# Cached latent pages on two halves of the stationary columns, with half-page transfers

## The reference

```python
# page: 128 positions; 32 pages for each of 8 samples; 16 heads; latent 256, rotary 32
ckv_past = cache_ckv[layer, page_table].reshape(bd, past, KV_LORA)
kr_past = cache_krope[layer, page_table].reshape(bd, past, QK_ROPE)
s_past = latent_scores(q_lat, q_rope, ckv_past, kr_past)   # (q_lat.ckv + q_rope.kr) * SCALE
s_new = latent_scores(q_lat, q_rope, c_kv, k_rope)         # the sample's own token
p = softmax(concatenate([s_past, s_new], axis=-1))
out = einsum(p[..., :past], ckv_past) + einsum(p[..., past:], c_kv)
```

## Time and profile before

| | |
|---|---|
| median of three runs | 938.44 us |
| profiled execution | 938.16 us, its span 936.5 us |
| TensorE busy | 896.2 us (96%) |
| VectorE, ScalarE, GpSimd busy | 481.7, 253.6, 97.0 us |
| DMA | 247.54 MB, mean 264 GB/s |
| mean granted TensorE clock | 0.991 |

### The profile page before, as it was taken

The page is one execution under the profiler, slowest core; times in us unless marked ns, Lnnn a source line. Parts: engine busy times, 40 slices in busy tenths (PEclk is TensorE's granted clock), DMA queues, the critical chain, the costliest instruction groups (busy, mean ns, idle before and its releaser), DMA issues.

```text
span 936.5 us, 13966 instructions
## 1 busy us (share of the span) xinstructions
PE 896.2 (96%) x5209; PEld 533.3 (57%) x5209; DVE 481.7 (51%) x1084; ACT 253.6 (27%) x553; POOL 97.0 (10%) x146
## 2 busy tenths in 40 slices
PE   8999999999999999999999999899999898897897
PEld 7777777677776755655678644444333333333443
DVE  2343778987753248677666446672111211014784
ACT  1122221032254125765720110221111111012346
POOL 0111211212112100000000000011211111011000
PEclk9999999999999999999999999999999999899999
DMA  9976988998897620101241495639999999999601
GB/s 374 363 253 242 340 289 294 324 385 314 286 360 277 241 75 20 49 20 43 99 186 64 185 425 243 237 122 401 425 421 422 425 421 425 424 417 351 239 24 68
DMA packets 65420, 247.54 MB, mean 264 GB/s; under 512 B 11301, under 2 KB 12078, under 8 KB 56358
## 3 DMA queue, kind: packets, MB, share of 16 engines
q1 hardware_dynamic: 46742, 191.41, 52.4%
q0 software_dynamic: 13216, 35.28, 10.2%
q10 hardware_dynamic: 5392, 19.93, 5.5%
HBM read 240.98 MB, written 18.05 MB: 277 GB/s over the span
## 4 chain that ended last, share of the span: by engine, by line
PE 78%; DMA 13%; DVE 5%; ACT 2%; issue 1%; SPq 1%; DVEq 0%; ACTq 0%; POOLq 0%
PE ps L1046 12%; DMA arena<-in_wexp 10%; PE ps L1538 9%; PE ps L997 8%; PE ps L1458 6%; PE ps L1382 4%; PE ps L1560 4%; PE ps L1133 3%; PE ps L1104 3%; PE ps L1218 3%; PE ps L1037 3%; PE ps L1663 2%; PE ps L1242 2%; PE ps L1182 2%; PE ps L1199 2%; PE ps L1108 1%
## 5 line engine op out<-in xcount | busy, mean ns | idle before, releaser
L1046 PE MATMUL ps<-arena 128*128 128x260 f32 x544 | 125.8, 387 | 1.9 <-DMA arena<-in_xT 1.0
L1046 PEld LDWEIGHTS ps<-arena 128*128 128x128 f32 x544 | 101.8, 191 | 22.9 <-issue 4.5
L2083 DVE SCALAR_TENSOR_TENSOR arena<-arena,vec 128x512 f32<-128x512 f32 x120 | 81.8, 746 | 0.0
L997 PE MATMUL ps<-arena 128*128 128x260 f32 x336 | 78.5, 387 | 0.1
L2935 POOL DMA_DIRECT2D arena<-in_kv x96 | 51.9, 542 | 252.1 <-issue 247.9
L2760 DVE TENSOR_TENSOR arena<-ps,arena 128x256 f32<-128x256 f32 x18 | 7.6, 425 | 129.6 <-ACT arena L1933 129.6
L1538 PE MATMUL ps<-arena 128*64 128x512 f32 x288 | 66.4, 615 | 7.3 <-DMA arena<-in_wexp 6.2
L997 PEld LDWEIGHTS ps<-arena 128*128 128x128 f32 x336 | 62.1, 190 | 12.9 <-issue 3.2
L1538 PE MATMUL ps<-arena,con 128*64 128x512 f32 x288 | 65.7, 609 | 3.7 <-DMA arena<-in_wexp 3.7
L1560 PE MATMUL ps<-arena 128*64 128x512 f32 x288 | 65.1, 593 | 3.7 <-DMA arena<-in_wexp 3.7
L1458 PE MATMUL ps<-arena 128*128 128x512 f32 x128 | 58.0, 600 | 0.0
(11 more groups left out here) (415 smaller groups left out, 1305.0 us busy)
## 6 DMA issues: line engine op xcount, KB each, us to landing
arena<-in_wexp SPq DMA_DIRECT2D x26, 2048.0 KB, 24.4
arena<-in_kv SPq DMA_DIRECT2D x160, 272.0 KB, 9.2
arena<-in_wexp SPq DMA_DIRECT2D x36, 1024.0 KB, 27.4
arena<-in_kv POOLq DMA_DIRECT2D x96, 272.0 KB, 7.5
arena<-in_w ACTq DMA_DIRECT2D x35, 512.0 KB, 8.2
arena<-in_wexp SPq DMA_DIRECT2D x16, 512.0 KB, 4.4
arena<-in_wo SPq DMA_DIRECT2D x8, 512.0 KB, 4.5
arena<-in_w_out SPq DMA_DIRECT2D x4, 1024.0 KB, 7.2
```

What stands on the lines that cost most here:

```text
L997: y = mm(ps[:, paired_bank(p, n), 0:TH], left(k), right(k), start=(k == 0), stop=(k == KD // 2 - 1))
L1046: y = mm(ps[:, b + h, 0:TH], w[:, k], xT[:, k, h * TH:(h + 1) * TH], start=(k == 0), stop=(k == KD - 1))
L2083: y = v.scalar_tensor_tensor(out=aT[:, c, 0:NPR], in0=win, scalar=wt, in1=aT[:, c, 0:NPR], op0=ALU.mult, op1=ALU.add)
```

## The change

Four pages of a sample are now laid on two **sides**. The 32 stationary columns of a sample hold its 16 heads twice, in columns 0 to 15 of one variant (side 0) and 16 to 31 of the other (side 1), each with zeros in the other half. Pages 0 and 1 of the four are scored with side 0 and pages 2 and 3 with side 1, into the same 256 columns of PSUM, so rows 0 to 15 of a sample's block hold two pages and rows 16 to 31 the other two. Scores, exponential and transposes are 256 wide. Values give for each row both sides' sums, 512 wide; the wrong half is not used, and the two right halves are added after the turning (`olT`). Each half of the rows has its own maximum and sum; a permutation `swap`, built from the identity by two copies, carries them over in two small matmuls at the end.

A page in memory is now 64 rows of 1088 numbers: row p, the rotary keys of two of the four position blocks each (64 numbers), row 64+p. It comes in two transfers, one to partitions 0 to 63 and one to 64 to 127, of 2048 and 2304 bytes a row; the longer one brings the rotary keys, to the lower partitions for pages 0 and 1 of four and to the upper for pages 2 and 3. So one rotary matmul contracts over the keys of both sides.

The core of the diff:

```diff
+ROW, HALF = 2 * P + KVL, P // 2
+SIDES, HH = 2, 16
...
+        def half_of(j, h):
+            return slice(h * ROW, (h + 1) * ROW + HALF) if h == j % 4 // 2 else slice(h * (ROW + HALF), h * (ROW + HALF) + ROW)
+        def page_half(n, j, h):
+            b, u = divmod(j, 4)
+            x = u // 2
+            first = x * (ROW + HALF)
+            place = slice(first - HALF * x * h, first + ROW + HALF * (1 - x) * (1 - h))
+            return rec[HALF * h:HALF * (h + 1), n % 2, b, u % 2, place]
...
-                    sp.dma_start(rec[:, n % 2, j], a["kv"][bass.ds(pg, 1)].rearrange("a p n -> (a p) n")
-                                 ).then_inc(s_kv[n % 2], 16)
+                    for h in range(2):
+                        sp.dma_start(page_half(n, j, h), a["kv"][bass.ds(pg, 1), :, half_of(j, h)].rearrange("a p n -> (a p) n")
+                                     ).then_inc(s_kv[n % 2], 16)
...
             def k_step(n):
-                pe.wait_ge(s_kv[s], 16 * SPN * (n // 2 + 1))
-                pe.wait_ge(s_kvp[s], 16 * (STEPS - SPN) * (n // 2 + 1))
+                pe.wait_ge(s_kv[s], 32 * SPN * (n // 2 + 1))
+                pe.wait_ge(s_kvp[s], 32 * (STEPS - SPN) * (n // 2 + 1))
                 for c in range(KKV):
+                    for x in range(SIDES):
+                        for bb in range(4):
+                            mm(ps[32 * bb:32 * bb + 32, bank, 0:2 * P], qlat[:, c, x, 4 * r + bb, :],
+                               rec[:, s, bb, :, x * (ROW + HALF) + c * P:x * (ROW + HALF) + (c + 1) * P], start=(c == 0 and x == 0), stop=False)
+                for j in range(2):
                     for bb in range(4):
-                        mm(ps[32 * bb:32 * bb + 32, bank, :], qlat[:, c, 4 * r + bb, :], kvr[:, s, bb, :, c * P:(c + 1) * P],
-                           start=(c == 0), stop=False)
-                for j in range(4):
-                    for bb in range(4):
-                        y = mm(ps[32 * bb:32 * bb + 32, bank, :].rearrange("p (u j i) -> p j u i", u=4, j=4)[:, j],
-                               qrz[:, j, 4 * r + bb, :], kvr[:, s, bb, :, 2 * P:2 * P + 32], start=False, stop=(j == 3))
+                        y = mm(ps[32 * bb:32 * bb + 32, bank, 0:2 * P].rearrange("p (u j i) -> p j u i", u=2, j=2)[:, j],
+                               qrz[:, j, 4 * r + bb, :], rec[:, s, bb, :, ROW:ROW + HALF], start=False, stop=(j == 1))
...
             def k_turn(n):
-                for u in range(4):
+                for u in range(2):
...
             def v_step(n):
-                for u in range(4):
-                    for bb in range(4):
-                        y = mm(ps[32 * bb:32 * bb + 32, 7, 0:KVL], pts[:, s, u * P + 32 * bb:u * P + 32 * bb + 32],
-                               kvr[:, s, bb, u, 2 * P + 32:REC], start=(u == 0), stop=(u == 3))
+                for x in range(SIDES):
+                    for u in range(2):
+                        for bb in range(4):
+                            y = mm(ps[32 * bb:32 * bb + 32, 7, x * KVL:(x + 1) * KVL], pts[:, s, u * P + 32 * bb:u * P + 32 * bb + 32],
+                                   rec[:, s, bb, u, x * (ROW + HALF) + 2 * P:x * (ROW + HALF) + ROW],
+                                   start=(u == 0), stop=(u == 1))
...
             def scores(p, s, x):
-                    pe.wait_ge(s_new, 3)
+                    pe.wait_ge(s_new, 7)
...
             def own_scores(r):
                 if r == 0:
+                    mm(ps[:, 4, 2:4], swap, negm[:].rearrange("p (r g) -> p r g", r=2)[:, :, 7], start=True, stop=True)
...
+                        for x in range(SIDES):
+                            mm(ps[32 * bb:32 * bb + 32, 4, r:r + 1], qlat[:, c, x, b, :],
+                               hT[:, B_CKV + c, NPR + b:NPR + b + 1], start=(c == 0 and x == 0), stop=False)
+            def own_sums():
+                pe.wait_ge(s_new, 5)
+                mm(ps[:, 4, 4:6], swap, fin[:, 10:12], start=True, stop=True).then_inc(s_cs, 1)
...
             def out_turn():
+                for x in range(SIDES):
+                    for r in range(2):
+                        for c in range(KKV):
+                            y = tr(ps[:, 6 + x, (2 * r + c) * P:(2 * r + c + 1) * P],
+                                   osum[r][:, (KKV * x + c) * P:(KKV * x + c + 1) * P], ident)
...
             gen_r(0)
+            own_sums()
             gen_v(0, 0)
...
             summed(STEPS - 1)
+            own_weights()
+            out_r(0, (0,))
             own()
-            out_r(0, (0, 1))
             out_v(0, 0)
...
-                    v.tensor_copy(olT.rearrange("p r c n -> p (r c n)"), ps[:, 6, :]).then_inc(s_olt, 1)
-                    out_r(0, (2, 3))
+                    v.tensor_copy(both, sides[0]).then_inc(s_olt, 1)
+                    dve.wait_ge(s_olt, 1)
+                    v.tensor_tensor(both, sides[1], both, ALU.add).then_inc(s_olt, 1)
+                    out_r(0, (1, 2, 3))
```

More of the change, by code:

```diff
@@ L409, in decoder_layer @@
         qlt = at(A_P, 1024)
[L410 to L420, removed]
+        qlat = at(A_QLAT, SIDES * KKV * NS * 32).rearrange("p (c x b h) -> p c x b h", c=KKV, x=SIDES, b=NS)
+        qrz = at(A_QRZ, 2 * NS * 32).rearrange("p (j b h) -> p j b h", j=2, b=NS)
+        rec = at(A_KV, 2 * STEPS * REC).rearrange("p (s b u n) -> p s b u n", s=2, b=4, u=2)
+        prb = at(A_P, 512).rearrange("p (s n) -> p s n", s=2)
+        pts = at(A_PTS, 512).rearrange("p (s n) -> p s n", s=2)
+        swap = at(A_SWAP, P)
+        osum = [at(off, SIDES * KVL) for off in (A_O, A_O2)]
+        olT = at(A_OLT, 256).rearrange("p (r c n) -> p r c n", r=2, c=KKV)
         wuv = at(A_W1R + 2048, 2048).rearrange("p (c n) -> p c n", c=KKV)
@@ L2048, in _ @@
             v.memset(fin[:], 0.0).then_inc(s_ini, 1)
+            v.memset(krs[:], 0.0).then_inc(s_ini, 1)
             dve.wait_ge(s_ini, N_INI)
@@ L2270, in _ @@
                     for c in range(KKV):
-                        v.tensor_copy(qlat[:, c, :, 0:HEADS].rearrange("p b (j i) -> p b j i", j=4), lat[:, c, 0:NS]
-                                      ).then_inc(s_qd, 1)
+                        for x in range(SIDES):
+                            v.tensor_copy(qlat[:, c, x, :, HH * x:HH * (x + 1)].rearrange("p b (j i) -> p b j i", j=4), lat[:, c, 0:NS]
+                                          ).then_inc(s_qd, 1)
+                    halves = [y.rearrange("p (b x h) -> p b x h", x=SIDES, h=HH) for y in (swap, ident)]
+                    for x in range(SIDES):
+                        v.tensor_copy(halves[0][:, :, x], halves[1][:, :, 1 - x]).then_inc(s_qd, 1)
                 if kind == "pw":
@@ L2381, in out_p, with own_weights @@
                                   ps[:, 5, c0:c0 + (i + 1) * P].rearrange("p (j q) -> p j q", q=P)).then_inc(s_td, 1)
-            def own():
-                last = negm[:].rearrange("p (r g) -> p r g", r=2)[:, :, 7]
-                lpast = lsum[:].rearrange("p (r g) -> p r g", r=2)[:, :, 7]
+            last = negm[:].rearrange("p (r g) -> p r g", r=2)[:, :, 7]
+            lpast = lsum[:].rearrange("p (r g) -> p r g", r=2)[:, :, 7]
+            def own_weights():
                 dve.wait_ge(s_cs, 2)
@@ L2414, in _ @@
+                dve.wait_ge(s_new, 12)
+                for r in range(2):
+                    y = v.scalar_tensor_tensor(out=osum[r][:, 0:KVL], in0=ps[:, 5, r * KVL:(r + 1) * KVL], scalar=fin[:, 16 + r:17 + r],
+                                               in1=osum[r][:, 0:KVL], op0=ALU.mult, op1=ALU.add)
+                y.then_inc(s_fin, 1)
             dve.wait_ge(s_cs, 1)
             v.tensor_copy(ckvs[:], ps[0:NS, 2, 0:KVL]).then_inc(s_cse, 1)
-            v.tensor_copy(krs[:], hT[64:96, B_KR, NPR:T]).then_inc(s_cse, 1)
+            for x in range(SIDES):
+                v.tensor_copy(krs[64 * x:64 * x + 32, :], hT[64:96, B_KR, NPR:T]).then_inc(s_cse, 1)
@@ L2424, in _ @@
                 if p == 0:
-                    dve.wait_ge(s_cs, 3)
-                    v.tensor_copy(olT.rearrange("p r c n -> p (r c n)"), ps[:, 6, :]).then_inc(s_olt, 1)
-                    out_r(0, (2, 3))
+                    dve.wait_ge(s_cs, 4)
+                    sides = [ps[:, 6 + x, :].rearrange("p (n x h) -> p n x h", x=SIDES, h=HH)[:, :, x] for x in range(SIDES)]
+                    both = at(A_OLT, 256).rearrange("p (n h) -> p n h", h=HH)
+                    v.tensor_copy(both, sides[0]).then_inc(s_olt, 1)
+                    dve.wait_ge(s_olt, 1)
+                    v.tensor_tensor(both, sides[1], both, ALU.add).then_inc(s_olt, 1)
+                    out_r(0, (1, 2, 3))
                 else:
@@ L2934, in step_pages @@
                     pg = pool.snap(numbers[j], min_val=0, max_val=NPOOL - 1)
-                    pool.dma_start(rec[:, n % 2, SPN + j], a["kv"][bass.ds(pg, 1)].rearrange("a p n -> (a p) n")
-                                   ).then_inc(s_kvp[n % 2], 16)
+                    for h in range(2):
```

(3 more changed lines are left out.)

73 lines of the change are left out of this document (36 added, 37 removed).

## The result

The changed kernel takes 1007.9 us, the median of four runs (1005.9 to 1015.4), beside 938.3 us (937.7 to 938.5) for the kernel before: 1.076 times as long, with an interval of 1.070 to 1.081. It is 70 us slower. The profiled execution took 1008.39 us.

The account below looks back on a forecast made before the run. Bounds: TensorE's list and, nearly equal behind it, the pages. From 938.2 us, TensorE's steps -13.3 and the own part +4.0 (together -9.3), then +16.9 for late pages, gave 945.8 us; range 928 to 1000 us.

Parts of the forecast that it names:

- The bound: Whole kernel: TensorE busy 96% of the span; behind it the pages, with DMA engines 88% busy from 62 to 320 us.
- serial rival: Page transfers: only one half of the partitions takes bytes at a time, 208 GB/s, 1031 us; chance 0.18, or near.
- the factor for a transfer to 64 partitions: Page transfers: engine time 1.19 times as much, 2.4 us more a step; 1.30 as upper value, giving 961 us.
- slacks: Steps 2 to 15, pages landing before scores start: 0.1 to 5.5 us each; each short by 3.2 us, shortfalls adding 16.9 us.
- TensorE's steps: Sixteen page steps: rotary matmuls save 8.5 us, transposes 4.85 us, together 13.3 us; latent scores and values unchanged.
- The own part: Samples' own row after the last step: 4.0 us added, from scores 1.7, swaps 0.2, transposes 0.6 and VectorE's chain 1.5.
- VectorE's longer chain: Samples' own row: VectorE comes to the second head's rotary products about 1.5 us later than TensorE.
- forecast case: Page transfers at a factor of 1.15 to 1.35, own range 940 to 970 us; chance 0.37.
- faster rival: Page transfers: halves cost the engines nothing, slacks fall short only in steps 6, 7 and 12, 930.6 us; chance 0.35.

Follow-up runs that it names:

- e10: Kernel before, with GpSimd's six pages of sixteen each in three transfers, rows 0 to 63, 64 to 95 and 96 to 127: 966.8 us, ratio 1.033.
- e11: Kernel before, with GpSimd's six pages each in three transfers, rows 32 to 95, 0 to 31 and 96 to 127: 949.2 us, ratio 1.013.
- e3: Kernel before, with only GpSimd's six pages of sixteen cut into two transfers of 64 rows: 973.3 us, ratio 1.037.
- e1: Kernel before, with each page in two transfers of 64 rows of 2176 bytes, nothing else changed: 999.9 us, ratio 1.063.
- e5: Changed kernel, with SyncE bringing the lower halves of all sixteen pages and GpSimd the upper ones: 989.1 us, ratio 1.052 against the kernel before.
- e8: Changed kernel with latents in 128-row transfers, separate rotary keys, eight pages per queue, and no value columns from step 2 on: 927.1 us.
- e9: Kernel before, with pages from step 2 on brought without their 256 value columns: 937.7 us, ratio 0.9991.

## Why the prediction was right and wrong

**The bound, right.** It had two nearly equal bounds, TensorE's list and the pages behind it, and put the cost where it fell: on the DMA engines, in TensorE's idle time before the scores. Most signs it named are there: share 0.97 (0.95 or more was named), landings of 11.2 us in the median on SyncE's queue (8.3 on GpSimd's; 11 and more was named), page packets dearer for a byte (1.42 times in engine time, below), idle time before the scores. But that idle time is 65.7 us and not 15 to 20, and two signs of the serial rival are there too, as told below.

**The step that failed: the factor for a transfer to 64 partitions.** I took 1.19 from one load of eight rows, with 1.30 from a store as the upper value. That load was eight packets in a window of 0.3 us, with a DMA share of 0.33, and it could not stand for queues that are full of half transfers. The store beside it showed 2.9, and I set it aside because pages are loads. Nor does the price go by the number of rows, along which I took the fourth root of 2.9: e10 and e11 have the same rows and differ. In the steps, with the engines full, the factor is 1.4: 360 to 259 GB/s for a unit of engine time over all traffic. For the two queues that bring the pages it is (0.523 + 0.295) x 328 / ((0.479 + 0.255) x 258) = 268 / 189 = 1.42, from the shares of SyncE's and GpSimd's queues after and the earlier trace rows, of the same stretch as the windows:

```profile
q1 hardware_dynamic: 24981, 43.47, 52.3%
q0 software_dynamic: 8388, 24.32, 29.5%
q10 hardware_dynamic: 3888, 14.16, 14.8%
```

**A second one in the same step: the price was put on the pages alone.** The third line is the weights, whose 3888 packets and 14.16 MB are the same as before. They take 0.148 x 328 = 48.5 us of the engines' time instead of 0.140 x 258 = 36.1, 1.34 times as much, though no weight transfer was touched. e3 shows the like on whole pages. So half transfers also make dearer what other queues bring; by what mechanism, no run here tells.

**And the slacks were the wrong sum once the engines are full.** I added shortfalls against 34 us of slack. With 1.42 in it, that sum has each slack short by 12.5 x 0.42 + 0.83 = 6.1 us and gives some 980 us: somewhat over half of the miss of 62 us is the factor, and the rest lies in the sum and in the traffic that it left out. Simpler, and nearer: a step had 0.88 x 17.0 = 15.0 us of engine time, so there were 2.0 us of room, which is used up at a factor of 1.14 on all traffic. Times 1.39, the factor over all traffic, it is 20.9 us, and at a share of 0.97 that is 21.5, near the 22.0 us between the steps. There the engines set the pace and TensorE's list does not: e1, with the old and longer list, is not slower than the changed kernel.

**Serial halves.** This rival said 208 GB/s for pages, 21.4 us a step for pages alone, and 1031 us. The time is 1008, much nearer to it than to the forecast, and the signs that I had named for it are there: a step's 4.46 MB of pages in 22.0 us are 203 GB/s, and the steps are 22.0 us apart. Still the halves aren't strictly one at a time. These 22.0 us hold the weights as well, and for a unit of engine time the two page queues move 253 GB/s, not half of the 355 before. In e5, with a queue for each half, the steps are 20.8 us apart (81.20 to 371.84), which is 215 GB/s of pages, above the 208; and e11, with its 64 rows across the middle of the partitions, is 19 us better than e10, with 64 rows below it.

The two halves run between one at a time and full speed: 253 GB/s for a unit of engine time, between the 355 of whole pages and half of it. And e5's split over two queues goes with 19 us less. I gave this rival 0.18 and held against it a load in a window of 0.3 us. That was the misjudgement behind the number.

**TensorE's steps: 13.3 us predicted, 10.4 measured** (e8, e9). Latent scores and values cost what they did, 30.9 us each, as predicted. A rotary part of two groups is 9.9 / 16 = 0.62 us a step, not half of 1.06; two transposes are 0.39 us, not 0.30. The prediction halved busy times, and these hold the last matmul's end, which overlaps the next group and isn't halved. From its first start to the start of the next group, the rotary part of the last step takes 0.98 us before and 0.55 after, the transposes 0.43 and 0.22; their busy times are 1.06 and 0.62 us, and 0.60 and 0.38, so the ends are 0.08 and 0.07 us, and 0.17 and 0.16.

**The own part: 4.0 us predicted, about 0.5 measured.** From the start of the last step's latent scores to the first matmul behind the samples' turned output (L1182 before, at 354.68 us, and L1203 after, at 423.44) it is 36.08 us before and 35.96 after, though that step's rotary scores and transposes are 0.6 us shorter. TensorE's timeline shows the swap matmul and the first own scores from 400.77 us on, and the next matmul at 402.04:

```profile
400.77 0.28 PE L1288 MATMUL ps<-negm,arena 128*128 128x2 f32 x2
400.98 0.44 PE L1293 MATMUL ps<-arena 128*32 128x1 f32 x10
...
401.91 0.20 PE L1295 MATMUL ps<-krs,arena 128*32 128x1 f32 x2
...
410.50 0.28 PE L1300 MATMUL ps<-fin,arena 128*128 128x2 f32 x2
...
414.67 1.06 PE L1314 MATMUL ps<-con,arena 128*128 128x128 f32 x8
...
419.10 2.43 PE L1239 MATMUL ps<-arena 128*128 128x128 f32 x8 [0.79 <-DVE arena L2381]
```

Twice as many own latent scores take 1.27 us with the swap, where the first block of four samples took 1.45 (it starts at 332.63, and the next matmul at 334.08). I had priced each group by the pitch of the old ones, which alternated between 128 rows and 32; now all are 128 rows high and lie closer together. That the height is the reason was not tried. VectorE's longer chain is late once, by 0.8 us, before the second head, where I had put 1.5. The two mis-sized terms nearly cancel: -13.3 + 4.0 = -9.3 us was forecast without the transfers, and -10.6 measured. That this sum is so near is luck.

**The clock, not in the prediction at all.** Latent scores took 41.9 us instead of 30.9 and rotary scores 12.4 instead of 9.9 (e8), 13.5 us together. The window from 105 to 108 us shows a granted clock of 0.50 behind one long wait. Behind the waits of 4.48, 6.02, 11.87 and 15.60 us it is 0.62, 0.54, 0.50 and 0.50 (windows from 145.74, 184.28, 234.35 and 369.43 us), and the records take 2.98, 3.46, 3.64 and 3.64 us; where no wait stands before them, from 125.88 and 164.65 us, it is 1.00 and they take 1.94 and 1.93. The stretch's busy time of 262.3 us stands against about 256.2 - 10 = 246 without that, so some 14 to 16 us of TensorE's time are the clock's, as an estimate. Whether they also lengthen the steps, by releasing buffers later, or only fill what would else be waiting, no run here tells apart; with the DMA engines at 0.97 there is little room for the former.

**The chances.** Slower had 0.55, and was right. That the forecast case (0.37) and the faster rival (0.35) were almost even came from the 1.19.

**Left open.** The changed kernel is 8 us slower than e1, by intervals of the ratio that do not meet (1.058 to 1.067 and 1.070 to 1.081), although its TensorE work is shorter and both have the same number of transfers. The unequal halves of 2304 and 2048 bytes are a candidate; they were not tried alone.

## What to carry to other kernels

Before cutting a transfer, read the DMA share of the stretch that it runs in and divide: the share of 0.88 here left a factor of 1.14 over all traffic. If a block has to come in two, cut it by columns (3 us here) or so that the large pieces have rows on both sides of partition 64, not into an upper and a lower half (61 us). And take the price of a kind of transfer from a stretch where the engines are busy: the one short load here gave 1.19, the steps 1.4.

## What the runs showed of the hardware

- Transfers within one half of the partitions bring the core's sixteen DMA engines, with the other traffic beside them, to a share of 1.01 at 255 GB/s (e1), where the mix before had 360 GB/s for a unit of engine time; with every lower half on one queue and every upper half on the other it is 264 GB/s at a share of 1.02 (e5).
- What runs beside them gets dearer: weights by a factor of 1.34 in engine time (the changed kernel), and whole pages on another queue land after 13.3 us instead of 9.0 (e3). So six pages of sixteen cost more than half of what sixteen cost, 34 of 61 us.
- Large pieces of 64 rows across the middle or below it differ by some 19 us for six pages a step (e11, e10).
- After a wait of 9.45 us the clock is granted at 0.50 and the 32 records of a step's latent scores take 3.64 us; without a wait before them it is 1.00, and they take 1.93 (the changed kernel).
